# First FFN pass of a DiT block: seven-product tiles from the fifth tile on, after four plain ones

## The reference

```python
for i in range(2):
    sh1, sc1, gt1, sh2, sc2, gt2 = silu(c) @ mod_w[i] + mod_b[i]      # the same for ctx from c_ctx
    x = x + gt1 * rms_norm(mixer_i(modulate(x, norm_g[i, 0], sh1, sc1)))
    h = rms_norm(x, norm_g[i, 2]) * (1 + sc2) + sh2
    u, g = split(h @ ffn_w_in[i])                                      # 2 x 2816 columns
    g = dwconv3x3(g, ffn_conv_w[i]) + ffn_conv_b[i]
    x = x + gt2 * rms_norm((silu(g) * u) @ ffn_w_out[i])
    # in layer 0 ctx takes the same path with the grid 1 x 256
```

## Time and profile before

| | us |
|---|---|
| time, three runs | 2444.37, 2446.18, 2445.93; median 2445.93 |
| profiled execution | 2442.24 |
| its span | 2440.1 |
| PE busy | 2348.6 (96%) |
| DVE / POOL / ACT busy | 1664.9 / 890.5 / 823.8 (68 / 36 / 34%) |
| mean granted clock | 0.986 |

### The profile page before, as it was taken

One profiled execution on the slowest core, in us unless ns is written; L12 is line 12 of the kernel. 1 busy time (PEld: TensorE's weight loads), 2 busy tenths in 40 slices (PEclk: granted clock), 3 DMA queues, 4 the chain that ended last, 5 costly groups with the idle time before them and its releaser, 6 DMA issues.

```text
span 2440.1 us, 35918 instructions
## 1 busy us (share of the span) xinstructions
PE 2348.6 (96%) x13630; PEld 1921.2 (79%) x13630; DVE 1664.9 (68%) x2143; ACT 823.8 (34%) x1203; POOL 890.5 (36%) x445
## 2 busy tenths in 40 slices
PE   7989999999999999999999998979999999999996
PEld 5557777877777788999889997767777888888884
DVE  4477888888888884543353325733577777889986
ACT  3642111211121115564443323333553333333332
POOL 0012121212121215664231104630486666666653
PEclk9999999999999999999999999989999999999998
DMA  8651112221222144653121228822211111111213
GB/s 346 235 199 78 73 56 86 86 84 45 86 86 86 43 198 153 220 181 137 55 78 57 67 73 236 215 95 70 69 52 53 52 52 52 52 60 69 69 44 138
DMA packets 106689, 255.09 MB, mean 105 GB/s; under 512 B 8928, under 2 KB 62816, under 8 KB 92128
## 3 DMA queue, kind: packets, MB, share of 16 engines
q1 hardware_dynamic: 89024, 228.56, 27.1%
q10 hardware_dynamic: 17568, 25.17, 2.8%
HBM read 223.68 MB, written 30.02 MB: 104 GB/s over the span
## 4 chain that ended last, share of the span: by engine, by line
PE 86%; DVE 5%; ACT 3%; POOL 3%; issue 2%; DMA 2%; SPq 0%; ACTq 0%; DVEq 0%; POOLq 0%
PE ps L739 18%; PE ps L740 17%; PE ps L741 17%; PE ps L1376 5%; PE ps L1378 5%; PE ps L1377 5%; PE ps L1125 2%; PE ps L1127 2%; PE ps L1126 2%; PE ps L1278 1%; PE ps L841 1%; PE ps L874 1%; PE ps L776 1%; PE ps L792 1%; PE ps L1016 1%
## 5 line engine op out<-in xcount | busy, mean ns | idle before, releaser
L3052 POOL TENSOR_TENSOR w_lo<-raw,w_hi 128x2048 fp32r<-128x2048 f32 x57 | 266.8, 4680 | 651.4 <-ACT w_hi L1644 291.3
L739 PE MATMUL ps<-hx_hi,w_hi 128*128 128x512 f32 x848 | 338.7, 399 | 2.4 <-ACT mix_out_c L1798 1.0
L740 PE MATMUL ps<-hx_hi,w_lo 128*128 128x512 f32 x848 | 331.7, 391 | 0.0
L741 PE MATMUL ps<-hx_lo,w_hi 128*128 128x512 f32 x848 | 331.4, 391 | 0.0
L2454 DVE TENSOR_TENSOR y_x<-y_x,ps 128x1024 f32<-128x1024 f32 x176 | 214.7, 1221 | 62.1 <-PE ps L741 58.5
L2436 DVE SCALAR_TENSOR_TENSOR acc<-ps,fcv,acc 128x945 f32<-128x945 f32 (+2 forms) x176 | 215.0, 1222 | 37.5 <-ACT acc L1688 16.4
L2954 DVE TENSOR_TENSOR y_x<-y_x,ps 128x512 f32<-128x512 f32 x304 | 206.8, 687 | 39.4 <-PE ps L741 39.4
L2906 DVE SCALAR_TENSOR_TENSOR acc<-ps,fcv,acc 128x945 f32<-128x945 f32 (+2 forms) x176 | 215.0, 1222 | 15.4 <-ACT acc L2102 2.3
L739 PEld LDWEIGHTS ps<-hx_hi,w_hi 128*128 128x128 f32 x848 | 160.0, 189 | 40.3 <-DVE hx_lo L2593 2.5
L741 PEld LDWEIGHTS ps<-hx_lo,w_hi 128*128 128x128 f32 x848 | 160.0, 189 | 34.1
L740 PEld LDWEIGHTS ps<-hx_hi,w_lo 128*128 128x128 f32 x848 | 160.2, 189 | 30.5
(11 more groups left out here) (415 smaller groups left out, 5611.2 us busy)
## 6 DMA issues: line engine op xcount, KB each, us to landing
raw<-in_ffn_w SPq DMA_DIRECT2D x44, 1024.0 KB, 6.6
modw<-in_modw SPq DMA_DIRECT2D x48, 512.0 KB, 7.1
raw<-in_ffn_w SPq DMA_DIRECT2D x44, 512.0 KB, 5.9
f_raw<-in_ffn_w SPq DMA_DIRECT2D x22, 1024.0 KB, 5.1
modw<-in_modw SPq DMA_DIRECT2D x21, 1024.0 KB, 4.8
raw<-in_mlstm_w SPq DMA_DIRECT2D x14, 1024.0 KB, 5.4
fw_raw<-in_ffn_w SPq DMA_DIRECT2D x22, 512.0 KB, 3.7
vch<-v_scr SPq DMA_DIRECT2D x18, 512.0 KB, 4.3
```

Of the source, the lines that this page charges most:

```text
L739: pe.matmul(out, whi, hhi, start=first, stop=False)
L740: pe.matmul(out, wlo, hhi, start=False, stop=False)
L741: return pe.matmul(out, whi, hlo, start=False, stop=last)
L3052: pool.tensor_tensor(w_lo[:, slot, 0:2048], raw[:, slot, 0:2048], w_hi[:, slot, 0:2048].bitcast(F32), ALU.subtract)\
```

## The change

The first pass (layer 0) has 4 plain tiles (`M`) and then 18 tiles of seven products.

- The functions of the seven-product tile are taken out of the second pass and made to serve both, through a class `Seven` with the semaphores' offsets and the places of the moving side of each pass (`FIRST`, `SECOND`). `FIRST` borrows semaphores that are idle by then; at the end VectorE sets seven counters on by `sem_inc`.
- Before the pass GpSimd makes five sums of quarters of h into `y_x`, where the memset was, and ScalarE adds the shift to eight blocks, ahead of its part of `ffn`. SP writes them out (`t_scr`, 4 x 1 MB) as soon as they are made, ahead of the loads of modulation and tile 2; VectorE's first `add` waits for these stores and copies in place of adding. They come back as t1 to t4 into places that the plain tiles leave free.
- Modulation chunks 0 to 2 are made as before. Chunks 3 to 20 are made on TensorE: `first_rows`, twice per tile, 4 matmuls of 128x32 by 256 (8 records each in a trace), and `first_columns`, 2 matmuls of two columns (4 records). Each half of a chunk (512 KB, `modh`) is loaded by SP after the rows of the half before. ScalarE copies a row and the columns out.
- Tile 4 is the transition, tile 5 its continuation, tiles 6 to 21 the steady ones. At the end VectorE's taps of tile 21 stand behind all sums of tile 20; `ctx_in(0)` waits for them.

```diff
-                project_first(None)
-                with pe.Fori(0, FT // 2 - 1) as i:
-                    project_in(i * 2 + 1, 1, i * 2)
-                    project_out(i * 2, 0)
...
+                for j in range(1, M):
+                    project_in(j, j % 2, j - 1)
+                    project_out(j - 1, (j - 1) % 2)
...
+            def first_rows(j, h):
+                pe.wait_ge(sem("modw1_in"), j * 32 + (16 * (M - 1) - 32 * M + 16 * h + 16))
+                for g in range(4):
+                    mm = pe.matmul(ps[32 * g:32 * g + 32, BANK_C, 0:MODW], c_pad[:, KH * h + g, :], modh[:, g, :],
+                                   start=(h == 0), stop=(h == 1), tile_position=(0, 32 * g), skip_group_check=True)
+                mm.then_inc(sem("modw_used"), 1)
+            def first_columns():
+                for b in range(2):
+                    mm = pe.matmul(ps[:, BANK_C, MODW + 2 * b:MODW + 2 * b + 2], mod_row[:, P * b:P * b + P], fold[:],
...
+            def third_first(j):
+                if S.first:
+                    pe.wait_ge(sem("a_done"), M)
+                    pe.wait_ge(sem("y_added"), 8 * M)
...
+                for name in ("g1", "g2"):
+                    product(name, j * 7 + (S["lo_in"] + S.made_at(True, name)), True)
...
+            ffn(p0, lows["x_pre2"])
+            third_first(M)
+            down(M - 1, (M - 1) % 2, old=True)
+            products(M, third=True)
+            with pe.Fori(0, (FT - 2 - M) // 2) as i:
+                products(i * 2 + (M + 1))
+                down(i * 2 + M, 0)
+                products(i * 2 + (M + 2))
+                down(i * 2 + (M + 1), 1)
+            products(FT - 1)
+            down(FT - 2, 0)
...
+            first_columns().then_inc(sem("modcol1_ready"), 1)
+            first_of_ctx()
+            down(FT - 1, 1)
```

On SP (the loads), ScalarE and VectorE:

```diff
+                sp.wait_ge(sem("first_low"), 13)
+                for i, (rows, ts) in enumerate(((0, 0), (1, 1), (0, 1), (1, 0))):
+                    sp.dma_start(t_scr[i], y_x[:, KH * rows:KH * rows + KH, TH * ts:TH * ts + TH]).then_inc(sem("t_out"), 16)
+                for j in range(1, M - 1):
+                    load_mod(j)
+                    tile(j + 1, a["ffn_w"][j + 1], (j + 1) % 2)
...
+                rows_done(M, 0)
+                first_mod_half(M - 1, 1)
+                halves_in(M + 1)
+                rows_done(M, 1)
+                first_mod_half(M, 0)
+                with sp.Fori(0, (FT - 2 - M) // 2) as i:
+                    for e in range(2):
+                        j = i * 2 + (M + 1 + e)
+                        halves_in(i * 2 + (M + 2 + e))
+                        out_in(i * 2 + (M + e))
+                        rows_done(j, 0)
+                        first_mod_half(i * 2 + (M + e), 1)
+                        rows_done(j, 1)
+                        first_mod_half(j, 0)
...
+                sp.wait_ge(sem("first_used"), FIRST["w_in_used"] + 7 * FT)
+                tile_out(K_FFNC, a["ffn_w"][0], K_FFNC % 2)
+                tile(K_FFNC + 1, a["ffn_w"][1], (K_FFNC + 1) % 2)
...
+            S = FIRST
+            for k in range(KT):
+                act.wait_ge(sem("first_low"), 10)
+                y = y_x[:, (k + KH) % KT, TH:TX]
+                act.activation(y, y, ACT.Identity, bias=shift(0, 1, "x", (k + KH) % KT)).then_inc(sem("t_shifted"), 1)
             ffn(p0, ctx_squares, ctx_split)
...
+                if third and S.first:
+                    gate_moved()
+                    part_high("s4", j, True)
+                    t4_high(0)
+                    up_moved()
...
+                    finish(j, par, gate_first)
+                    for name in ("g1", "s1", "s2", "s4", "s3", "g2", "u2"):
+                        part_high(name, j + 1)
...
+            t4_low(0)
+            gate_first_half(M, True)
+            f_add(M - 1)
+            gate_second(M, True)
+            t4_low(1)
+            up_second(M, 0, True)
+            with dve.Fori(0, (FT - 2 - M) // 2) as i:
+                f_tile(i * 2 + (M + 1), 1)
+                f_tile(i * 2 + (M + 2), 0)
+            f_tile(FT - 1, 1)
...
+            f_taps(FT - 1)
+            f_gate(FT - 1, 1)
+            f_add(FT - 1, among_last_sums)
```

More of the change, by code:

```diff
@@ L546, in load_mod, with halves_in @@
                 sp.dma_start(modw1[:], a["modw1"][c]).then_inc(sem("modw1_in"), 16)
[L548 to L553, removed]
[L554 to L556 removed]
+            def halves_in(j):
+                sp.wait_ge(S.sem("lo_in"), j * 7 + S["lo_in"])
+                sp.dma_start(f_raw[:], a["ffn_w"][j + S.w0][:, 0:2048]).then_inc(S.sem("raw_in0"), 16)
@@ L575, in _ @@
             tile(1, a["ffn_w"][1], 1)
[L576 to L582, removed]
+            the_rest()
             for h in range(2):
@@ L1100, in _, with product @@
             pe.wait_ge(sem("cmix_out"), KT)
+            def product(name, made, third=False, low=None):
+                pe.wait_ge(S.sem("lo_in"), made)
+                q, p = MOVING[name], S.slot(third, name)
+                out = ps[:, PRODUCT_BANK[name], :]
+                for k in range(KH):
+                    if low is not None and k % 2 == 0:
+                        by, count = low[k // 2]
+                        pe.wait_ge(sem(by), count)
+                    ws = slice(P * k, P * k + P)
+                    pe.matmul(out, p_hi[p][:, ws], S.x(q, k)[0], start=(k == 0 and name in ("g1", "g2", "s1")), stop=False, skip_group_check=True)
+                    pe.matmul(out, p_lo[p][:, ws], S.x(q, k)[0], start=False, stop=False, skip_group_check=True)
+                    mm = pe.matmul(out, p_hi[p][:, ws], S.x(q, k)[1], start=False, stop=(k == KH - 1), skip_group_check=True)
+                mm.then_inc(S.sem("w_in_used"), 1)
@@ L1461, in down @@
[L1461 to L1473 removed]
+            S = SECOND
@@ new lines, in f_gate @@
+            def f_gate(j, par):
+                dve.wait_ge(sem("silu_done"), j + (S["silu_done"] + 1))
+                dve.wait_ge(sem("act_moved"), PLAIN_MOVED + 3 if isinstance(j, int) and j == 0 and not S.first else j * 4 + (S["act_moved"] + 4))
+                if S.first or not (isinstance(j, int) and j < PLAIN):
+                    dve.wait_ge(sem("dve_moved"), j * 3 + (S["dve_moved"] + 3))
+                dve.tensor_tensor(fprod[:, par, :], acc[:], fprod[:, par, :], ALU.mult).then_inc(sem("a_done"), 1)
@@ new lines, in parts @@
+            def parts(j, par, fourth=False):
+                if fourth and not S.first:
+                    gated_low(j - 2, par)
+                    out_low(j - 2)
+                part_low("g1", j)
+                if not fourth:
+                    out_low(j - 2)
+                part_sum("s1", j)
+                part_sum("s2", j)
+                part_low("s1", j)
+                part_sum("s4", j)
+                if not fourth:
+                    gated_low(j - 2, par)
+                part_low("s2", j)
+                part_low("s4", j)
+                part_sum("s3", j)
+                part_low("s3", j)
+                part_low("g2", j)
+                part_low("u2", j)
```

847 lines of the change are left out of this document (503 added, 344 removed).

## The result

| | before | changed |
|---|---|---|
| median, 20 runs each | 2443.56 us | 2447.77 us |
| ratio | | 1.0015, 95% interval 1.0009 to 1.0021 |
| profiled execution, span | 2440.1 us | 2443.5 us |

The account below looks back on a forecast made before the run. TensorE, busy 96% of the span, was taken to bound the kernel. Steady tiles −43.8, startup +5.9, transition +17.1 and end +20.5 sum to −0.3 on 2442.2; with 3.7 to the median, 2445.5 us, range 2432 to 2458.

Parts of the forecast that it names:

- the transition: Tiles 3 to 5, up to tile 6's start: TensorE waits and half clock cost +17.1 us, bounds +6 and +24.
- the steady tiles: Tiles 6 to 21: 34.63 us each becomes 31.89, saving 2.74 each, −43.8 us in all, bounds −51 to −38.
- the end: After down(20): context products wait for tile 21's taps, later loads delay squares; +20.5 us, bounds +14 and +26.
- Part 2: Startup: ScalarE's shifts delay macc, stores and loads slow hc_scr; +5.9 us, bounds +3 and +10, the larger ruled out.
- The second wait at the seam: Tile 5, before its rows: modulation half queued on SP behind halves_in(6) lands at +96.6, another 5 us idle.
- Part 3: The transition's step-by-step timing from tile 3's input products to tile 6, at T+121.0 against T+103.9: +17.1 us.
- Part 4: The end's timing: TensorE idle 12.1 us before ctx_in(0), first sums at E+39.4, 1 for clock; +20.5 us.
- the 1.86 of the row products: Steady tiles: rows in two breaks of 0.70 us each and four column records at 0.46 cost 1.86 per tile.
- A: Tile-5 seam costs only 2.8 + 1.7 us because SP reaches the load earlier; 2438, or 2432 with end's lower bound; chance 0.30.
- B: Steady tiles: modulation half lands after the rows want it, excess over 3 us slack times 16; 2455 at 0.6 over; 0.14.
- C: Edges worse together than apart, startup at +10 and end at +26: 2455 us; chance 0.15.
- D: Steady tiles as slow as before, breaks costing 4 us and not 1.86 by stopping weight loads: 2480; chance 0.05.

Follow-up runs that it names:

- e1: Changed kernel, but SP issues the loads of modulation chunk 1 and tile 2 before waiting for GpSimd's sums: 2439.02 us, 0.9987 of the kernel before.
- e2: As e1, with shifts between the context's squares, stores after hc_scr landed and GpSimd's last two sums later: 2445.75 us, 1.0010 of the kernel before.
- e7: As e6, with four of ScalarE's eight shifts moved ahead of the last modulation row: 2427.86 us, 0.9945 of the kernel before.
- e3: Changed kernel, but for tile 5 alone SP issues the second modulation half before tile 6's load: 2444.96 us, 1.0002 of the kernel before.
- e4: Changed kernel with the orders of SP, ScalarE and GpSimd rearranged at the tile 4 to 6 seam: 2435.95 us, 0.9972 of the kernel before.
- e8: Changed kernel with one of four 128x32 row products per break, the other three left out: 2444.8 us in one run.
- e9: As e7, but GpSimd's last two sums wait until VectorE has made all eight blocks of the context's input: 2420.49 us, 0.9902 of the kernel before.
- e6: Changed kernel with e1, e4 and earlier context-tile and res_x loads plus reordered ScalarE at the end: 2419.35 us, 0.9912 of the kernel before.

## Why the prediction was wrong

The forecast was 2445.5 us, no change; the time lay 0.15% above the kernel before. Three of the four terms were near: the transition (+17.1, measured +18.0, its single waits within 0.3 us of their forecast times), the steady tiles (−43.8, measured −42.6) and the end (+20.5, measured +20.0). That the forecast of the time, 2445.5, lies only 2.3 below the measured 2447.77 flatters it: my base was the median of three runs, 2.4 above that of twenty (2443.56). As a difference I had −0.4 and the runs show +3.7.

The step that failed is a term of Part 2: "sharing the engines adds perhaps 1.3 there and 1.3 at the xc_scr stores". The whole startup, +9.7, is 0.5 for a modulation load that came later, 2.9 for the shifts (I had 3.0), 0.7 up to the issue of hc_scr (a wait of VectorE for an xc_scr store, 0.98, is in it), 5.0 for hc_scr itself (11.3 us, not 6.3) and 0.5 of clock. So sharing cost 5.7 where I had 2.6. These 3.1 us are most of the 3.7 by which the sum of −0.3 missed the 3.4 between the spans, and without them there would be next to no difference; the other lines of the ledger make up the rest (+0.7 startup, +0.8, +0.9, +1.2, −0.5 and −2.5). The mechanism, sharing with SP's queue, was right, and e1 shows it: with SP's loads out of the way hc_scr takes 6.2 us again and the kernel is 6.8 us faster. The size was wrong.

The Trainium skill (DMA: Bandwidth & Descriptors, section "Queues, rings and completion order") says that a DMA engine goes round the queues that have work for it, a packet at a time. If two full queues share alike, a transfer takes about twice its 6.3 us alone, 12.6 as an estimate; the 11.3 measured agrees, since SP's queue had 1.74 MB left against 2.10. I had used the rule to rule out the larger bound and not to work out the term.

Part 2 also has "The new GpSimd sums take the place of a memset and are hidden as it was". TensorE's time was not touched by it in the changed kernel, but VectorE was: two blocks stood for 4 us each, and e2 and e7 lost 6 and 8 us to this.

Some things were half right. The second wait at the seam, in tile 5, was laid to SP's queue alone; e3 shows that ScalarE's order held the same moment. With e4 both waits of tile 5 all but go: 11.4 of the 18.0 us of the transition were the order of the queues and not a price of the method. In Part 3 the step from +56.95 to +75.6 does not add up: 60 matmuls at 0.227 and the 1.86 are 15.5, not 18.7; the trace has 17.3 (+56.7 to +74.0), with waits of 0.78 and 0.86 in it. In Part 4 two misses cancel: TensorE stood 10.6 us and not 12.1, and the first sums came at E+38.0 and not +39.4, but the half clock behind them cost 2 and not 1. And the 1.86 of the row products stands although its price per record falls (e8).

Of the rivals, A's mechanism (the half not late) did not occur; B fell with 487.00 of 487.00 us busy; C came nearest with its startup of +10, but its end of +26 did not come; D fell by the period of 31.96. The range, 2432 to 2458, held the time; the chances of 0.37 for faster against 0.30 for slower leaned the wrong way.

## What to carry to other kernels

A cheaper inner loop pays at its edges what its order costs: price each edge by the instruction that the next one waits for on each queue, and look for a second cause that ends at the same moment before crediting the removal of the first. When a second DMA queue is full, add to a transfer the time of the bytes that the other queue moves beside it, up to the transfer's own time again (11.3 in place of 6.3 us here); issue loads that nobody needs yet well before the one on the path, as e1 does. When an operation of another engine takes the place of one that read nothing, ask what it reads, and which engine's operations run beside it. Here reordering three edges turned a change that lost 0.15% into one that gains 0.9%, with the same arithmetic.

## What the runs showed of the hardware

- A VectorE operation with both inputs in SBUF stood still for a whole GpSimd operation: 4.36 to 4.43 us for blocks of 0.41 and 0.48 (2.13 for one that began in the middle of a sum), beside GpSimd's 128x2048 sums of 4.6 us (changed kernel, e2, e7), and 0.41 again where they are apart (e9). The taps, which read one input from PSUM, kept their 1.25 beside the same sums (7 in 8.8 us in e9). One operation that began just before a sum was not held (1.21 us at 163.86 in e6, the sum at 163.89). The Trainium skill (SBUF — State Buffer, section "Who interferes with whom") says that a VectorE instruction with two SBUF inputs contends with a GpSimd instruction that reads SBUF, not with one that only writes. The trace agrees: beside the memset of the kernel before, which reads nothing, the blocks took 0.41 to 0.42.
- Four 128x32 products in four column groups cost what one costs (e8, 31.92 against 31.96 a tile). A break of the stream with one such round costs 0.78 us, with two rounds 1.22.
